# Value products of the second attention: two heads into the two halves of one bank, taken pair by pair

## The reference, cut to what matters

```python
# fox_attention: causal, with a forget term added to the logits
s = jnp.einsum('bhqd,bhkd->bhqk', qb, k) * scale + cq[..., :, None] - c[:, :, None, :]
p = jax.nn.softmax(jnp.where(mask, s, NEG_INF), axis=-1)
o = jnp.einsum('bhqk,bhkd->bhqd', p, v)
# dilated_attention: causal, three patterns of keys mixed by their softmax denominators
w = jax.nn.softmax(jnp.stack(lses, axis=0), axis=0)
o = jnp.sum(w[..., None] * jnp.stack(outs, axis=0), axis=0)
```

## Time and profile before

| | |
|---|---|
| median of 3 runs | 2333.74 us (2330.88 to 2334.06) |
| span of the profiled execution | 2330.9 us |
| TensorE busy, share of the span | 97% |
| VectorE, ScalarE, GpSimd busy | 55%, 39%, 54% |
| mean granted TensorE clock | 0.991 of full speed |
| the 16 heads of the second attention | from 761 to 938 us |

### The profile page before, as it was taken

How to read it: one execution, slowest core, us unless ns; L and a number is a source line. 1 busy time by engine, 2 the same in 40 slices (tenths; PEclk the granted TensorE clock), 3 DMA queues, 4 the chain that set the end, 5 groups by cost and what they waited for, 6 DMA issues and landing times.

```text
span 2330.9 us, 29683 instructions
## 1 busy us (share of the span) xinstructions
PE 2250.9 (97%) x9663; PEld 1762.8 (76%) x9670; DVE 1289.9 (55%) x2379; ACT 903.1 (39%) x1427; POOL 1252.0 (54%) x807
## 2 busy tenths in 40 slices
PE   7999899999999999899999999999999999999998
PEld 5666566677767676688888888888887888888887
DVE  5454323214751457588667666322222888888887
ACT  4554444335543444433333333322222333333333
POOL 3432022234534221328888888888887656556553
PEclk9999999999999999999999999999999999999999
DMA  6664123333522110223666666666556899999996
GB/s 234 200 203 148 51 85 104 100 100 132 176 73 83 54 46 28 91 78 64 144 149 142 146 146 148 141 144 145 108 106 161 319 326 349 360 349 354 351 358 243
DMA packets 238226, 392.71 MB, mean 168 GB/s; under 512 B 87201, under 2 KB 161953, under 8 KB 237889
## 3 DMA queue, kind: packets, MB, share of 16 engines
q1 hardware_dynamic: 159808, 324.29, 42.8%
q0 software_dynamic: 78336, 67.45, 14.4%
HBM read 330.60 MB, written 61.01 MB: 168 GB/s over the span
## 4 chain that ended last, share of the span: by engine, by line
PE 56%; DVE 2%; DMA 1%; ACT 0%; issue 0%; POOL 0%; SPq 0%; DVEq 0%; POOLq 0%; ACTq 0%
PE bank L1377 30%; PE bank L1388 22%; PE bank L1149 4%; PE bank L1360 0%; DMA tail<-hidden_of_last_block,low 0%; ACT staged L1428 0%; DMA tail<-gates 0%; DMA hidden_of_last_block<-staged 0%; DVE u_split L2157 0%; DVE low L1863 0%; POOL tail L1076 0%; DVE tail L2089 0%; DVE tail L2124 0%; DVE tail L2122 0%; DVE tail L2125 0%
## 5 line engine op out<-in xcount | busy, mean ns | idle before, releaser
L1028 POOL DMA_INDIRECT gates<-low x384 | 631.9, 1646 | 140.2 <-issue 116.7
L1377 PE MATMUL bank<-h_high,u_tiles_split 128*128 128x512 f32 x2048 | 631.9, 390 | 2.2 <-DVE u_tiles_split L2056 2.2
L1000 POOL TENSOR_TENSOR u_split<-blocks,u_split 128x1024 fp32r<-128x1024 f32 (+1 forms) x102 | 245.0, 2402 | 658.2 <-ACT u_split L1532 625.4
L1149 PE MATMUL bank<-h_high,u_split 128*128 128x512 f32 x1664 | 547.2, 404 | 11.8 <-DVE h_low L1885 7.7
L1388 PE MATMUL bank<-v_split,a_split 128*128 128x512 f32 x2286 | 520.1, 390 | 3.3 <-DVE a_split L2196 3.3
L1388 PEld LDWEIGHTS bank<-v_split,a_split 128*128 128x128 f32 x2286 | 430.0, 188 | 93.4 <-DVE v_split L2193 4.1
L1377 PEld LDWEIGHTS bank<-h_high,u_tiles_split 128*128 128x128 f32 x2048 | 385.3, 188 | 82.4 <-issue 2.4
L1377 PE MATMUL bank<-h_low,u_tiles_split 128*128 128x512 f32 x1024 | 399.1, 390 | 0.0
L1149 PEld LDWEIGHTS bank<-h_high,u_split 128*128 128x128 f32 x1664 | 316.0, 190 | 89.3 <-issue 22.7
L2056 DVE TENSOR_TENSOR u_tiles_split<-tail,u_tiles_split 128x1024 fp32r<-128x1024 f32 x128 | 157.3, 1230 | 362.9 <-ACT u_tiles_split L1713 362.0
L1149 PE MATMUL bank<-h_low,u_split 128*128 128x512 f32 (+1 forms) x704 | 277.2, 394 | 0.0
(11 more groups left out here) (219 smaller groups left out, 2366.6 us busy)
## 6 DMA issues: line engine op xcount, KB each, us to landing
tail<-in_uT SPq DMA_DIRECT2D x128, 512.0 KB, 3.8
tail<-in_v SPq DMA_DIRECT2D x128, 512.0 KB, 5.7
gates<-blocks SPq DMA_DIRECT2D x32, 768.0 KB, 5.8
tail<-gates SPq DMA_DIRECT2D x128, 192.0 KB, 5.7
kept_hidden<-tail SPq DMA_DIRECT2D x96, 192.0 KB, 1.9
tail<-kept_hidden SPq DMA_DIRECT2D x96, 192.0 KB, 6.4
blocks<-in_r SPq DMA_DIRECT2D x24, 512.0 KB, 4.1
blocks<-in_conv SPq DMA_DIRECT2D x16, 512.0 KB, 4.4
```

Source lines behind the costliest of these rows:

```text
L1000: nc.gpsimd.tensor_tensor(flat(u, 1)[:, 0:n], ring[:, loads[0] % NW, 0:n], flat(u, 0)[:, 0:n].bitcast(F32), ALU.subtract).then_inc(s_wlo, 1)
L1028: nc.gpsimd.indirect_dma_start(gate_elements, bass.IndirectOffsetOnAxis(ap=expert_no[tb][:, k:k + 1], axis=0), expert_gate[tb][:, k:k + 1] ...
L1149: last = mm(ps[0:m, :], flat(u, part)[:, k * m:(k + 1) * m], x, start=(k == 0 and j == 0), stop=(k == nk - 1 and j == 2))
L1377: last = mm(bank[slot % 2][:, :], U4[:, slot, w, k, :], x[:, k, :], start=(k == 0 and x is hh and w == 0), stop=(k == KD - 1 and w == 1))
```

## The change

For heads 12 to 27, `PV` no longer uses the weights of both heads. Each head's product has its own 64 columns of values as weights and writes its own half of `ob`: rows 0 to 63 for an even head, rows 64 to 127 for an odd one. The products leave the loop over blocks. They are taken for both heads of a pair during the odd head, alternating: after X and S of i = 2, PV(a-1, 0), PV(a, 0), PV(a-1, 1), PV(a, 1); and at the end of the odd head the same for key blocks 2 and 3. An even head has no value product at all. The transposed probabilities of an even head stay in `PT` and those of an odd head in a second buffer `PT_odd`, one slot for each key block, so eight slots; a slot waits for the product of the head two before. `O` runs once for each pair and copies all 128 rows. In the projection-free and piece-wise heads the order is otherwise as it was. The step `L` is dropped.

```diff
+    def value_pair(a, kb0, kb1):
+        for kb in range(kb0, kb1):
+            STEPS.append(("PV", a - 1, kb))
+            STEPS.append(("PV", a, kb))
...
             if j + 1 < ATT2:
                 STEPS.append(("S", a + 1, i))
-            STEPS.append(("L", a, i))
-            if i:
-                if j + 1 < ATT2:
-                    STEPS.append(("W", a + 1, i - 1))
-                STEPS.append(("PV", a, i - 1))
+            if i and j + 1 < ATT2:
+                STEPS.append(("W", a + 1, i - 1))
+            if i == 2 and j % 2:
+                value_pair(a, 0, 2)
...
             STEPS.append(("W", a + 1, TB - 1))
-        STEPS.append(("PV", a, TB - 1))
-        STEPS.append(("O", a))
+        if j % 2:
+            value_pair(a, 2, TB)
+            STEPS.append(("O", a))
...
+        PT_odd = region(HH + 6144, 4 * T, 4)
...
-                if kb == 0 and a > 0:
+                if kb == 0 and a >= 12:
+                    pe.wait_ge(s_O, O_no[a // 2 * 2 + 1] - 1)
+                elif kb == 0 and a > 0:
                     pe.wait_ge(s_O, O_no[a] - 1)
...
+                if a >= 12:
+                    r0 = DH * (a % 2)
+                    v = (VA if a < 20 else VB)[:, kb, (a - 12) % 8, :]
+                    mm(ob[r0:r0 + DH, c0:T], v, (PT, PT_odd)[a % 2][:, kb, c0:T],
+                       start=(kb == 0), stop=(kb == nk - 1)).then_inc(s_PV, 1)
+                    return
...
-                if x > 4:
+                if a >= 14:
+                    act.wait_ge(s_PV, pv_no[(a - 2, kb)])
+                elif a >= 12:
+                    act.wait_ge(s_PV, pv_no[(11, MB - 1)])
+                elif x > 4:
                     act.wait_ge(s_PV, x - 4)
...
             def O(a):
+                dve.wait_ge(s_PV, pv_no[(a, n_keys(a) - 1)])
+                if a >= HEADS:
+                    end(V.tensor_copy(oT[:, a if a < 12 else (a - 12) // 2, :], ob[:, :]), s_O, "s_O")
                     return
```

More of the change, by code:

```diff
@@ L1314, in PV @@
                 else:
-                    pair = (a if a < HEADS else (a - 12) % 8) // 2 * 2
-                    v = (VA if a < 20 else VB)[:, kb, pair:pair + 2, :].rearrange("p h d -> p (h d)")
+                    pair = a // 2 * 2
+                    v = VA[:, kb, pair:pair + 2, :].rearrange("p h d -> p (h d)")
                 mm(ob[:, c0:T], v, PT[:, slot, c0:T], start=(kb == 0), stop=(kb == nk - 1)).then_inc(s_PV, 1)
@@ L1626, in high_probs @@
                 act.wait_ge(s_X, x)
-                if x > 4:
+                if a >= 14:
[3 more added lines that the diff above has]
+                elif x > 4:
                     act.wait_ge(s_PV, x - 4)
                 c0 = q0(a, kb)
-                nc.scalar.copy(PT[:, (x - 1) % 4, c0:T], tile_bank[("X", a, kb)][:, c0:T]).then_inc(s_Ph, 1)
+                place_ = (PT, PT_odd)[a % 2][:, kb, c0:T] if a >= 12 else PT[:, (x - 1) % 4, c0:T]
+                nc.scalar.copy(place_, tile_bank[("X", a, kb)][:, c0:T]).then_inc(s_Ph, 1)
             def forget(n):
@@ L1969, in O @@
             def O(a):
-                if HEADS <= a < 12:
-                    dve.wait_ge(s_PV, pv_no[(a, n_keys(a) - 1)])
-                    end(V.tensor_copy(oT[:, a, :], ob[:, :]), s_O, "s_O")
+                dve.wait_ge(s_PV, pv_no[(a, n_keys(a) - 1)])
+                if a >= HEADS:
+                    end(V.tensor_copy(oT[:, a if a < 12 else (a - 12) // 2, :], ob[:, :]), s_O, "s_O")
                     return
[L1974 to L1977, removed]
+                r0 = DH * (a % 2)
+                end(V.tensor_copy(oT[r0:r0 + DH, a // 2, :], ob[r0:r0 + DH, :]), s_O, "s_O")
             def post(kind, i, ns):
```

## The result

The changed kernel takes 2321.80 us (median of 4 runs, 2313.65 to 2324.22) beside 2333.01 us (4 runs, 2330.88 to 2334.06): ratio 0.9949, 95% interval 0.9936 to 0.9961. The forecast was 2322.5, its direction "faster".

What follows compares the result with a forecast made beforehand. TensorE, busy 97% of the span, was taken as the bound. Six pairs saving 9.7 us and the last four heads 1.5 gave 11.2 us, so 2322.5 us from the median of 2333.74; 8-in-10 range 2317 to 2336.

Steps and rivals of the forecast that it cites:

- TensorE sets the length of a head, and the rest follows: Heads with a projection are bound by TensorE, even ones falling from 11.63 to 9.04 us; attention savings are handed on whole.
- The two halves overlap: In the odd head's product blocks, 64-column products in different array halves run at once, at least partly.
- rival (2): No overlap of the value products in the odd head: 0.8 us slower, 2334.5 us, no change; chance 0.28.
- Stagger: In the odd head's blocks, matmuls start in program order, so neighbours overlap only partly: 2.77 us per pair; chance 0.47.
- rival (1): Whole overlap in the odd head's blocks: 2.13 us per pair, 15.6 us saved, 2318.1 us; chance 0.14.
- Change-over: Entering and leaving 64-column weights at each product block costs 0.14 + 0.10, some 0.25 us per block, 0.5 per pair.
- Waits around the blocks: Scores of i = 2 need a bank that ScalarE empties, and TensorE reaches them early: 0.3 us charged per pair.
- rival (3): Each step between halves in a block costs a change-over: 2346.5 us at 0.25 us each, 2339.3 at 0.10; chance 0.11.
- j = 12 and j = 14: Projection-free heads: j = 12 gains perhaps 0.4 us by earlier eviction, j = 14 ends some 1.6 us earlier.
- j = 15: The last head takes over head 14's products, yet gets 0.5 us shorter.
- j = 13: In this head near the end VectorE's chain stays, so its length stays at 10.45 us: gain 0.
- rival (4): Longer pause ahead of j = 13 keeps the clock at 1.2 GHz longer: up to 1.5 us; no case of its own.

Runs made afterwards that it cites:

- the later cast: Changed kernel with ScalarE's cast of the next weights put off, which stood ahead of the copy that j = 0's scores wait for: 2318.45 us, ratio 0.9940.

## Why the prediction came out right, and where it was wrong

- **TensorE sets the length of a head, and the rest follows:** right for the head: even ones 9.11 us for 9.04, dilated ones 9.43. The rest took 1386.6 and 1386.8 us for 1385.4; 0.5 and 1.5 of that is a longer wait for the gates, which varies without following the gain, so the traces show no loss behind the stage that belongs to the change.
- **The two halves overlap:** right, and with both heads in one half the gain is gone. That kernel is rival (2) made real: it took 2336.6 us for the 2334.5 that the rival gave.
- **Stagger:** the first wrong step, the term of the sum that was priced too dear. "Starts keep program order: a1 a2 b1 b2" gave 2.77 us per pair. The products overlap wholly, 2.13 us, as rival (1) has it; two and two start together, and even with the other order of products.
- **Change-over:** "some 0.25 us per block" was right as it was read. Entering costs 0.09 us ahead of the block and 0.05 in its first step (0.48 for 0.43), leaving 0.10 (from 775.76 to 776.18 are 0.42 us for 0.32), the 0.14 + 0.10 of the earlier trace rows. Left out were the 0.06 us to the second transpose. Products and change-overs together: 2.13 + 0.62 = 2.75 us per pair for 3.27 of the forecast.
- **Waits around the blocks:** 0.4 us per pair for 0.3. 23.26 less 5.18 for the old products plus 2.75 for the new is 20.83; the pair takes 21.24. With one block for each pair it is 0.4 as well (23.26 - 5.18 + 2.13 + 0.31 = 20.52 for 20.92). Net: 2.0 us per pair, not 1.6.
- **Change-over at each step, rival (3):** refuted. The blocks have three steps between heads and 0.31 us in all, of which the part inside is as large with both heads in one half.
- **j = 12 and j = 14:** 0.38 and 1.80 us for 0.4 and 1.6: right. j = 15: 0 for 0.5.
- **j = 13:** the second wrong step. "Its length stays at 10.45: 0" looked at VectorE's chain and left the clock to rival (4) as "up to 1.5 us". The wait grew to 5.6 us, where some 5 were foreseen, and the head lost 2.37 us to the earlier trace rows and 3.7 to what it takes at the full clock, 9.08.
- **The sum:** 11.2 us. Measured in the stage 10.1, and 1.6 more without the chance of j = 0. About 2.2 too little was credited to the pairs and 2.4 too little charged to j = 13; they cancel.

## What to carry to other kernels

Two products that need only 64 columns each cost little more than one if they write different halves of the output and stand next to each other; collect them in as few blocks as the buffers allow, since each block costs a change-over (0.31 us here), and don't mind the order within. Read such a cost also in the steps ahead of the block and behind it: inside it only half of it showed. Work taken off the bounding engine in a stretch where another engine is the bound becomes a pause there, and a pause is not free: look at the granted clock of what comes next, and move useful work in. Price the two apart, for here a loss of 2.4 us hid behind a gain that had been priced too low by as much.

## What the runs showed of the hardware

- Float32 products of 64 columns in different column halves run wholly side by side: 1.65 us for eight matmuls that take 3.16 in one half. TensorE takes the second half's first matmul up although four of the first half (two products) stand ahead of it (block of 1.66 us, an estimated 2.67 in order).
- Going to 64 columns and back costs 0.31 us per block: 0.09 ahead of its first matmul, 0.16 to 0.18 inside it, overlap or not, and 0.06 behind the first matmul after it.
- The clock after a pause is not a function of the pause alone. It fell after each pause of 5.35 us or more, in 2 of 8 traces after 1.06 us, and in 6 of 12 after 2.78 us, with the same work on both sides of the wait; but in all 12 after a shorter one of 2.17 us (up to 1084 us in the changed kernel), and in none of 3 after 1.6 us. Such a fall costs 1.3 to 4.6 us (36.38 us for 35.08 behind the stage, and 13.71 for 9.08 in j = 13, both with the later cast), and can take back what was gained ahead of it.
